# Sixteen experts on one core: the token block is turned by TensorE in place of DMA transposes

## The reference

```python
cap = CAPACITY_FACTOR * n // N_EXPERTS              # 256 tokens for each of 16 experts
probs = jax.nn.softmax(logits, axis=-1)
gate, idx = lax.top_k(probs.transpose(0, 2, 1), cap)
xs = jax.vmap(lambda hb, ib: hb[ib])(h, idx)        # 256 rows of 1024 for each expert
hid = (jax.nn.silu(jnp.einsum('becd,edf->becf', xs, p['w_gate']))
       * jnp.einsum('becd,edf->becf', xs, p['w_up']))
out = jnp.einsum('becf,efd->becd', hid, p['w_down']) * gate[..., None]
y = jax.vmap(lambda ob, ib: jnp.zeros((n, d), ob.dtype).at[ib.reshape(-1)].add(ob.reshape(-1, d)))(out, idx)
```

## Time and profile before

| | |
|---|---|
| median of 3 runs | 2274.81 us (2272.99 to 2279.75) |
| the profiled execution, its own time | 2279.75 us |
| its span in the profile | 2278.0 us |
| granted TensorE clock, mean over the span | 0.973 |
| TensorE matmuls | busy 2149.4 us, 94% |
| VectorE | busy 1591.4 us, 70% |
| ScalarE | busy 1016.3 us, 45% |
| GpSimd | busy 505.1 us, 22% |

### The profile page before, as it was taken

The page is one execution under the profiler, slowest core; times in us unless marked ns, Lnnn a source line. Parts: engine busy times, 40 slices in busy tenths (PEclk is TensorE's granted clock), DMA queues, the critical chain, the costliest instruction groups (busy, mean ns, idle before and its releaser), DMA issues. The chain is left out here.

```text
span 2278.0 us, 37763 instructions
## 1 busy us (share of the span) xinstructions
PE 2149.4 (94%) x14437; PEld 1432.0 (63%) x14437; DVE 1591.4 (70%) x2204; ACT 1016.3 (45%) x1315; POOL 505.1 (22%) x538
## 2 busy tenths in 40 slices
PE   7799999999999999999975999999999999999995
PEld 3444444444878787845532777777777777777772
DVE  2749999885679787865566676666666667666666
ACT  3611002355666666555542444434444444443444
POOL 1710001012657676600004110111110111101111
PEclk9899999999999999999987999999999999999998
DMA  9341002355011211265544877778788887777886
GB/s 350 99 75 33 19 19 88 125 154 163 8 52 38 63 46 31 99 237 186 161 157 167 269 245 237 250 240 271 241 246 251 254 261 247 243 244 243 260 262 264
DMA packets 280292, 392.88 MB, mean 172 GB/s; under 512 B 101508, under 2 KB 142980, under 8 KB 279694
## 3 DMA queue, kind: packets, MB, share of 16 engines
q1 hardware_dynamic: 262062, 333.12, 44.5%
q0 software_dynamic: 16528, 56.47, 9.0%
q10 hardware_dynamic: 1616, 2.16, 0.3%
HBM read 313.44 MB, written 62.54 MB: 165 GB/s over the span
## 5 line engine op out<-in xcount | busy, mean ns | idle before, releaser
L89 PE MATMUL pgu<-xhi,mwhi 128*128 128x256 bf16 x2048 | 558.5, 273 | 0.0
L90 PE MATMUL pgu<-xlo,mwhi 128*128 128x256 bf16 x2048 | 558.4, 273 | 0.0
L91 PE MATMUL pgu<-xhi,mwlo 128*128 128x256 bf16 x2048 | 558.4, 273 | 0.0
L2483 DVE TENSOR_TENSOR mwlo<-mwst,mwhi 128x2048 bf16<-128x2048 f32 x187 | 427.0, 2284 | 0.0
L2383 ACT ACTIVATE mwhi<-mwst 128x2048 bf16<-128x2048 f32 x186 | 350.8, 1901 | 8.4 <-DMA mwst<-in_w_gate 8.4
L2391 ACT ACTIVATE thb<-pgu 128x256 f32<-128x256 f32 x128 | 49.0, 383 | 546.2 <-PE pgu L91 546.2
L676 DVE SCALAR_TENSOR_TENSOR co<-u,taps,co 128x1984 f32<-128x1984 f32 (+22 forms) x120 | 234.2, 1951 | 3.7
L2494 DVE SCALAR_TENSOR_TENSOR thb<-thb,pgu 128x256 f32<-128x256 f32 x128 | 53.8, 420 | 245.0 <-ACT thb L2391 245.0
L2318 POOL TENSOR_TENSOR mpflag<-mpflag 1x1 f32<-1x1 f32 x46 | 37.4, 813 | 819.1 <-DVE ysb L2510 552.5
L89 PEld LDWEIGHTS pgu<-xhi,mwhi 128*128 128x128 bf16 x2048 | 200.4, 98 | 24.9
L90 PEld LDWEIGHTS pgu<-xlo,mwhi 128*128 128x128 bf16 x2048 | 200.5, 98 | 24.4
(11 more groups left out here) (405 smaller groups left out, 4275.8 us busy)
## 6 DMA issues: line engine op xcount, KB each, us to landing
mwst<-in_w_gate SPq DMA_DIRECT2D x32, 2048.0 KB, 9.0
mwst<-in_w_up SPq DMA_DIRECT2D x32, 2048.0 KB, 8.1
mwst<-in_w_down SPq DMA_DIRECT2D x32, 2048.0 KB, 11.9
wst<-in_w_in SPq DMA_DIRECT2D x28, 512.0 KB, 6.1
big<-in_ada_w SPq DMA_DIRECT2D x5, 2048.0 KB, 14.1
s_rows<-row SPq DMA_DIRECT2D x16, 520.0 KB, 5.7
u<-in_ada_w SPq DMA_DIRECT2D x8, 1024.0 KB, 6.3
xt<-in_x SPq DMA_DIRECT2D x16, 512.0 KB, 4.4
```

The costliest lines, as they stand in the source:

```text
L89: nc.tensor.matmul(out, lh, rh, start=(first and k == 0), stop=False)
L90: nc.tensor.matmul(out, lh, rl, start=False, stop=False)
L91: ins = nc.tensor.matmul(out, ll, rh, start=False, stop=(last and k == n - 1))
L2483: nc.vector.tensor_tensor(wlo[:, b, ks], wst[:, b % NS, ks], whi[:, b, ks], ALU.subtract)\
```

## The change

For the experts 1 to 15 the DMA transposes and their waits are gone, and TensorE turns the block for every expert, as it did for expert 0. The first 16 transposes of expert e+1 stand after step f = 6 of expert e, the other 16 after step q = 0. ScalarE and VectorE each take two copies from PSUM for each expert, placed in `body` ahead of the weight splits that follow the first and the second q. The copies wait until all eight f of expert e are done, because those still read `xhi` and `xlo`. The gather of the next expert's rows waits for the transposes of the rows that it overwrites.

```diff
             @block.sync
-                def turned(e):
-                    wait(sp, gu_ps, e * 8)
-                    sp.sem_inc(x_free, 1)
-                    sp.wait_ge(x_free, 1)
-                    for part, x in enumerate((xhi, xlo)):
-                        for s in range(2):
-                            sp.dma_start_transpose(x[:, :, s * P:(s + 1) * P], rows[:, s, part * D:(part + 1) * D])\
-                                .then_inc(xt_in, 16)
...
-                        if b == (NS if first else NS - 1):
-                            wait(sp, got, e * 32 + 32)
+                        if b == NS and isinstance(e, int) and e == 0:
+                            wait(sp, got, 32)
                         wait(sp, w_lo[b % NS], 2 * (e * 2 + b // NS))
                         EW.load(sp, e, b)
-                        if b == NS - 1:
-                            turned(e)
...
             @block.gpsimd
-                    if not first:
-                        wait(pool, tx_ps, 4)
-                        wait(pool, xt_in, e * 64 - 64)
+                    wait(pool, tx_ps, e * 4)
...
             @block.scalar
-                def turn(j):
-                    wait(act, tx_ps, 2 * j + 1)
+                def turn(e, j):
+                    wait(act, tx_ps, e * 4 + 2 * j + 1)
+                    wait(act, gu_ps, e * 8)
                     nc.scalar.activation(xhi[:, 4 * j:4 * j + 4, :], ptx[0][:], ACT.Copy).then_inc(tx_ok[0], 1)
...
                     for q in range(4):
                         if nxt:
+                            if q < 2:
+                                turn(e + 1, q)
                             split(e, HEAD_START + 8 + q)
...
             @block.vector
-                def turn(j):
-                    wait(dve, tx_ps, 2 * j + 2)
+                def turn(e, j):
+                    wait(dve, tx_ps, e * 4 + 2 * j + 2)
+                    wait(dve, gu_ps, e * 8)
                     nc.vector.tensor_copy(xlo[:, 4 * j:4 * j + 4, :], ptx[1][:]).then_inc(tx_ok[1], 1)
...
                     for q in range(4):
                         if nxt:
+                            if q < 2:
+                                turn(e + 1, q)
                             split(e, HEAD_START - 1 + 8 + q)
...
             @block.tensor
-                def turn(j):
-                    wait(pe, got, 32)
+                def turn(e, j):
+                    wait(pe, got, e * 32 + 32)
                     for part in range(2):
-                        wait(pe, tx_ok[part], j)
+                        wait(pe, tx_ok[part], e * 2 + j)
                         for k in range(4):
                             for s in range(2):
...
                 def body(e, nxt):
                     start = isinstance(e, int) and e == 0
-                    if start:
-                        for part in range(2):
-                            wait(pe, tx_ok[part], 1)
-                    else:
-                        wait(pe, xt_in, e * 64)
+                    for part in range(2):
+                        wait(pe, tx_ok[part], e * 2 + (1 if start else 2))
...
                             token_list(e + 1)
+                        if nxt and f == 6:
+                            turn(e + 1, 0)
...
                         last.then_inc(d_ps, 1)
+                        if nxt and q == 0:
+                            turn(e + 1, 1)
```

More of the change, by code:

```diff
@@ L2244, in moe_stage @@
                                                       m.sem("idc_ok"), m.sem("gt_ok"))
-        got, tx_ps, tx_ok, xt_in = m.sem("got"), m.sem("tx_ps"), m.sems("tx_ok", 2), m.sem("xt_in")
-        x_free = m.sem("x_free")
+        got, tx_ps, tx_ok = m.sem("got"), m.sem("tx_ps"), m.sems("tx_ok", 2)
         gu_ps, mth_ok, sg_ok, hid_ok, fhi_ok, flo_ok = (m.sem("gu_ps"), m.sem("mth_ok"), m.sem("msg_ok"), m.sem("hid_ok"),
@@ L2274, in _ @@
             def _(sp):
-                def turned(e):
-                    wait(sp, gu_ps, e * 8)
-                    sp.sem_inc(x_free, 1)
-                    sp.wait_ge(x_free, 1)
-                    for part, x in enumerate((xhi, xlo)):
-                        for s in range(2):
-                            sp.dma_start_transpose(x[:, :, s * P:(s + 1) * P], rows[:, s, part * D:(part + 1) * D])\
-                                .then_inc(xt_in, 16)
                 def one(e):
-                    first = isinstance(e, int) and e == 0
                     for b in range(NB):
-                        if b < NS and first:
+                        if b < NS and isinstance(e, int) and e == 0:
                             continue
-                        if b == (NS if first else NS - 1):
-                            wait(sp, got, e * 32 + 32)
+                        if b == NS and isinstance(e, int) and e == 0:
+                            wait(sp, got, 32)
                         wait(sp, w_lo[b % NS], 2 * (e * 2 + b // NS))
                         EW.load(sp, e, b)
-                        if b == NS - 1:
-                            turned(e)
                 peeled(sp, NE, one)
@@ L2441, in prep0 @@
                 def prep0(e):
-                    turn(0)
-                    turn(1)
+                    turn(0, 0)
+                    turn(0, 1)
                 experts(act, prep0, body)
```

## The result

| | before | after |
|---|---|---|
| median | 2276.59 us (4 runs, 2272.99 to 2279.75) | 2303.64 us (4 runs, 2302.60 to 2305.76) |
| profiled execution, span | 2278.0 us | 2304.3 us |
| TensorE matmul instructions | 14437 | 14917 |

Between these medians the kernel after is slower by 27.05 us. The record has 18 runs of it in all, 2298.63 to 2306.00 us, with a median of 2302.18 us. Against 2276.59 us that is 25.6 us and the ratio 1.0112, with a 95% interval of 1.0099 to 1.0126, or 22.5 to 28.7 us. Ratios and intervals here count fast runs alone; one run of experiment 8, at 2420.47 us, was a slow one. The forecast was 26.8 us and 2301.6 us. The prediction started from 2274.81 us for the kernel before, whose median with one more run is 2276.59, so 1.8 of the 2.0 us between 2301.6 and 2303.64 are that shift and not the change. The range of 2296 to 2312 us holds the time.

What follows compares the result with a forecast made beforehand. TensorE's gapless stream was taken to bound the kernel. 480 transposes at 55.9 ns add 26.8 us, every other part nothing: 2274.81 + 26.8 = 2301.6 us, range 2296 to 2312 us.

Steps and rivals of the forecast that it cites:

- What bounds the kernel: Expert stage: TensorE, busy in all of an expert's 63.04 us, sets its length; relieving other engines or queues gives nothing.
- Part 1: TensorE's stream, experts 1 to 15: 480 added transposes at 55.9 ns cost 26.8 us (12.0 and 52.4 at the bounds).
- Part 2: First transpose group, after f = 6: gathered rows land about 6 us before TensorE needs them, so the wait costs nothing.
- Part 3: Second group, after q = 0: both first PSUM copies end in time, VectorE's 1.2 us early; costed at nothing.
- Part 4: Copies on ScalarE (2 x 1.02 us) and VectorE (2 x 0.69 us) per expert: both have room.
- Parts 5 and 6: SyncE's queue loses four DMA transposes per expert, next load about 2.6 us earlier; expert 0 and tail: all worth nothing.
- rival C: Expert start: freeing DMA queues ends a TensorE wait for the x block, not slower; 2.0 us wait gives 2272; chance 0.02.
- Rival A: After q = 0: copies come too late and TensorE waits, 15 x 1.1 = 16 us added, 2318; chance 0.06.
- Rival B: Transpose groups: they pull TensorE's granted clock down, 30 groups cost 39 us more, 2341; chance 0.03.
- rival D: TensorE's stream: a transpose costs only a token-list matmul's 25 ns, 12.0 us in all, 2286.8; chance 0.03.

Runs made afterwards that it cites:

- experiment 8: Kernel before with DMA transposes behind the fifth weight block, and the fourth and fifth blocks of experts 1 to 15 cut to an eighth: 2394.04 us, 1.0492.
- experiment 5: Kernel after with VectorE's two copies of each expert placed behind the weight split instead of ahead of it: 2323.20 us, 1.0208 of the kernel before.
- experiment 3: Kernel after with only one of eight transposes in experts 1 to 15, all waits and copies kept: 2279.56 us, 1.0017 of the kernel before.
- experiment 4: Kernel before without its 60 DMA transposes, experts 1 to 15 using expert 0's x block: 2275.78 us, 1.0004.
- experiments 6 and 7: Kernel before with DMA transposes of experts 1 to 15 behind the fifth (6: 2472.31 us) or fourth (7: 2323.21 us) weight block instead of the third.
- experiment 2: Kernel after with each transpose of experts 1 to 15 issued four times: 2381.60 us, 1.0466 of the kernel before.
- experiment 1: Kernel after with each transpose of experts 1 to 15 issued twice into the same place: 2329.34 us, 1.0229 of the kernel before.

## Why the prediction was right

The whole result is one term of its sum.

- **What bounds the kernel** held. TensorE's stream sets the length of an expert. Over 4, 16, 32, 64 and 128 transposes in an expert, its length is 63.26, 63.94, 64.83, 66.62 and 70.20 us: 55 to 56 ns for each above 63.04.
- **Part 1**, 55.9 ns for a transpose, came from a straight line through two prices in the trace of before. It measured 56 ns in the timeline and in the length of an expert (1.79 us / 32). The medians agree but say it less sharply: 27.05 us / 480 = 56.4 ns, and 25.6 us / 480 = 53.3 ns over all 18 runs. The bounds of 25 and 109 ns were far too wide for what the line knew. Wrong beside it was the duration of one: 219 ns, where 270 were named. Nothing hung on it.
- **Part 2**, the gather's cover, held: no wait on the gathered rows after expert 0.
- **Part 3**, the tight place, held to a tenth: 1.2 us of margin was predicted and is there, and experiment 5 shows by a wait of 1.1 us what lies behind it.
- **Part 4** held: experiment 3 has all copies and nearly no transposes, and lies within 1.6 to 6.4 us of before. ScalarE's split behind the second copy was forecast 7.15 us behind the mark of f = 7 and starts 6.54 us behind it, because that copy needs only the high part's eight transposes. Nothing hung on it.
- **Parts 5 and 6** held in what they said of this change. The load went out 2.7 us earlier (2.6 predicted), and experiment 4 puts its worth and that of the DMA transposes at nothing, within 0.15%. Weaker was the reasoning in rival C that the x block has over 8 us to spare. At its place it has. But experiments 6 and 7 show that this spare time can't be spent by moving the transposes back in the queue: they hold it for longer there, and experiment 8 lays that to the weight transfers beside them.
- **Rival A** did not happen, as no wait for a copy was added, but experiment 5 shows that its mechanism was real. Its price was put a little too low, at 16 us where the trace shows 19.2. **Rival B** fell in experiment 2, **rival C** in experiment 4, **rival D** in experiment 1.

No version beats the kernel before. The cheapest on TensorE is the one that leaves it out of the work, and taking the DMA transposes away as well (experiment 4) gains nothing more.

## What to carry to other kernels

Where one engine is busy without a gap through a stage, price a change by what it adds to that engine's stream, and look for nothing in return from the queues it relieves: here 480 short instructions at 56 ns gave 26.8 us, where the 15 experts of the trace grew by 26.9 and the medians by 25.6 to 27.05. Read the pace from marks on another engine's timeline (starts of the instruction that each step releases), not from durations, and fit it by size over two shapes. A margin that comes from a transfer's place in a queue holds for that place only; moving it one block back cost 47 us here.

## What the runs showed of the hardware

- At a granted clock of 1.00 transposes of 128x128 bf16 between matmuls start every 56 ns and last 219 ns; 64 in a row leave the clock at 1.00 (experiment 2).
- A stop of TensorE of 1.1 us cost 1.28 us, and one of 10.8 us cost 12.5 us: in the latter the clock's mean was 0.67 during the wait, and it was at 0.50 for at least 2.6 us after it.
- Four DMA transposes of one expert's block held the issuing queue for 9.1 us beside the third weight block, 10.0 to 13.6 us behind the fourth, and 15 us behind the fifth; with these two blocks cut to an eighth, 8.4 to 10.4 us.
